# Ways into two expert mixtures: clearing, spreading, selection and turned rows in another order

## The chip, the cores and the metric

The kernel runs on one core of one Trainium2 chip, in one launch. The metric is the device time of that launch in microseconds (us). The kernel before takes 2220.22 us, the median of three runs (2218.92 to 2225.36).

## The reference, cut to what matters

The input is 256 tokens of width 1024, all in float32. A first block has two layers: sparse attention with a dense feed-forward part, then block-wise attention with a mixture of 8 experts (width 3584, two chosen per token). A second block follows: an mLSTM and Fourier mixer, and a mixture of 16 experts (width 512, two chosen per token out of one group of four). What the change touches is how tokens get to their experts:

```python
logits = (xf @ w_router).astype(F32)                 # first mixture; the second adds a group choice
vals, idx = lax.top_k(logits, TOP_K_EXPERTS)
w = jax.nn.softmax(vals, axis=-1)
for e in range(N_EXPERTS):
    y = y + gate[:, e:e + 1].astype(xf.dtype) * swiglu(xf, wg[e], wu[e], wd[e])
...
x = x + gate2 * rmsnorm_2(hier_moe(h2, lp), g_post_ffn[l])
```

## The kernel before, in words

Activations are held transposed: 8 tiles of 128 channels by 256 tokens (`hT` is the residual stream, `uT` the normed input). Weights stream from HBM through six ring slots of 2 MB, all issued by SyncE in one fixed order. Every engine runs its own hand-written order, and they meet in semaphores.

A helper pair hands results from TensorE (PE) to the engine that takes them: `open_job` gives TensorE one of the five PSUM banks 1 to 5 in rotation, and waits until the job five before has been taken; `next_job` is the taker's side. `copy_job` is ScalarE's (ACT) copy of such a bank. `settle` makes TensorE wait until all jobs so far are taken.

The way into a mixture (`routing(m, X)`, for m = 0 and 1) is, on TensorE: four jobs `byt` of four transposes each (the normed tokens as rows, `by_token`); in the second mixture four more jobs `hR` (the residual `hT` turned to rows, `rows_h`, for the output's last step); then the job `rank` (five small matmuls that count the tokens ahead of each within its expert), for which VectorE (DVE) must have found the choices (`s_a`); then, when VectorE has the slot of each token (`s_lg`), two jobs `gr` of four matmuls each. The first spreads the slot columns `cols[54:58]` over the partitions, and ScalarE copies it to `grow`; the second spreads the weights `cols[46:50]`, for `wrow`. Then TensorE settles, and `zero_sums` clears the four banks 4 to 7, in which all outputs of the mixture are summed, by four matmuls with zeros.

VectorE meanwhile runs `top2`: choices, softmax weights, ranks, slots (up to L1917, `s_lg`), then the table of which expert each tile of slots belongs to (L1921 to L1929, `s_tab`). Then it enters the mixture: it copies the slot number (L1776, L1816) and makes `selection`, the 0/1 matrix `pick` (L1759, L1762) with which TensorE gathers the tokens of a tile (`gather`, L756). In the second mixture it then clears two tiles (L1818, L1819).

The mixture itself loops over tiles of slots (96 wide in the first, 64 in the second). Before its loop, TensorE waits for `s_tab` and `M.sel` and gathers; ScalarE and VectorE copy the gathered inputs to `xg` (`inputs`, L1410 and L1766); TensorE clears the two banks of the tile's own output (`clear_y`, L770, first mixture only) and starts on the gate weights (L776, or L870 in the second). Each of the first mixture's tiles takes seven chunks of 6 MB of weights, twelve granules each; SyncE loads a granule of the next chunk when TensorE is through with the one in its place. The second mixture's tiles take one chunk of 6 MB in three loads, each issued when the same slot's weights have been used. The first chunk of both is loaded ahead. SyncE, TensorE, ScalarE and VectorE each read the number of tiles from the table with `value_load`.

Ahead of the second mixture's router stand two norms in a row: squares by ScalarE, sums by TensorE (L518), root by ScalarE (L1318), reciprocal (L1625) and scaling (L1620) by VectorE, shift by ScalarE (L1331), and the router's matmuls (L713).

Of the kernel before, what the change touches and what calls it, by code (L numbers as in the profile page):

```python
# [14 lines left out]
P = 128  # L15
# [3 lines left out]
NT = T // P  # L19
# [55 lines left out]
def program(nc, A, out):  # L75
    with ExitStack() as ctx:
# [3 lines left out]
        def sem(name):  # L80
            return ctx.enter_context(nc.semaphore(name))
# [159 lines left out]
        s_top = sem("top_found"); s_e = sem("top_exponential"); s_lg = sem("gates_by_token")  # L241
        s_a = sem("choices_ready"); s_tab = sem("tables_ready")
# [224 lines left out]
        def _(pe):  # L467
# [232 lines left out]
            def zero_sums():  # L700

                for i in range(4):
                    pe.matmul(psum[:, 4 + i, :], zeros[:], pk("causal"), start=True, stop=False,
                              skip_group_check=True)

# [11 lines left out]
            def routing(m, X):  # L717
# [9 lines left out]
                if m == 1:  # L727
                    pe.wait_ge(s_hT, 28)
                    for t in range(NT):
                        for g in range(2):  # L730
                            b, _ = open_job(pe, "hR", "A")
                            for k in range(4):
                                mm = pe.transpose(b[:, P * k:P * k + P], hT[:, 4 * g + k, P * t:P * t + P], ident)
                            mm.then_inc(res, 1)
# [8 lines left out]
                pe.wait_ge(s_lg, m + 1)  # L743
                for o in (54, 46):
                    b, _ = open_job(pe, "gr", "A")
                    for q in range(4):
                        mm = pe.matmul(b[:, P * q:P * q + P], cols[:, o + q:o + q + 1].to_broadcast([P, P]), ident,
                                       start=True, stop=True)
                    mm.then_inc(res, 1)
# [11 lines left out]
            def first_mixture():  # L761
# [5 lines left out]
                def clear_y():  # L767

                    for i in range(2):
                        pe.matmul(psum[:, 2 + i, 0:4 * N], zeros[:], pk("causal")[:, 0:4 * N], start=True, stop=False,  # L770
                                  skip_group_check=True)
# [68 lines left out]
            def second_mixture():  # L840
# [16 lines left out]
                pe.wait_ge(s_tab, 2)  # L857
                pe.wait_ge(M.sel, 1)
                pe.wait_ge(*mark["byt"][-1])
                gather(M)  # L860
                last = pe.value_load(M.tab[0:1, TABLE:TABLE + 1], min_val=0, max_val=TABLE - 2)
# [236 lines left out]
            settle()  # L1098
            zero_sums()
# [180 lines left out]
            norm()  # L1280
            router(uT, "router2", 20, 56)
            routing(1, uT)
            settle()
            zero_sums()
# [18 lines left out]
        def _(act):  # L1303
# [18 lines left out]
            def h_pairs(v):  # L1322

                return lambda i: (s_hT, 4 * v - 3 + i)
# [69 lines left out]
            def routing(m):  # L1394
# [7 lines left out]
                if m == 1:  # L1402
                    for t in range(NT):
                        for g in range(2):
                            copy_job("hR", rows_h[:, t, 512 * g:512 * g + 512], lambda b: b)
                for dst in (grow, wrow):
                    copy_job("gr", dst, lambda b: b)
# [8 lines left out]
            def first_mixture():  # L1416
                M = mix[0]
                N, CH = M.N, M.CH
                last = act.value_load(M.tab[0:1, TABLE:TABLE + 1], min_val=0, max_val=TABLE - 2)
                act.wait_ge(M.gath, 1)  # L1420
                inputs(M)
                with act.Fori(0, last + 1) as q:
# [12 lines left out]
            def second_mixture():  # L1435
                M = mix[1]
                act.sem_inc(M.yA, 1)
                last = act.value_load(M.tab[0:1, TABLE:TABLE + 1], min_val=0, max_val=TABLE - 2)
                act.wait_ge(M.gath, 1)
                inputs(M)  # L1440
                with act.Fori(0, last + 1) as q:
# [76 lines left out]
            act.wait_ge(s_tab, 1)  # L1518
# [60 lines left out]
            norm(hT, h_pairs(7))  # L1579
# [918 lines left out]
```

## Time and profile before

| what | value |
|---|---|
| median of three runs | 2220.22 us |
| the profiled execution, its own time | 2222.7 us |
| its span in the profile | 2220.7 us |
| PE busy | 2059.9 us, 93% |
| DVE busy | 596.2 us, 27% |
| ACT busy | 406.2 us, 18% |
| DMA | 640.83 MB, mean 289 GB/s |
| mean granted TensorE clock | 0.964 of full |

Some 1.5 us or more lie outside the span: the profiled execution's own time is 2.0 us above it. Times in the timelines are us from the start of the span. A line of the timeline is start, duration, engine, line of the kernel, operation, what is written and read, the number of instructions merged in it, and in brackets how long the engine had been idle before and what released it. PE is TensorE's array, PEld its weight load, SPq SyncE's queue. The granted clock is a share of 2.4 GHz: 1.00 is the upper level, 0.50 the lower (1.2 GHz).

### The profile page before, as it was taken

How to read it: one execution, taken by the hardware profiler on the slowest of the kernel's cores; microseconds unless marked ns; L12 is line 12 of the kernel's file. 1: busy time of each engine (PE TensorE's matmuls, PEld its weight loads, DVE VectorE, ACT ScalarE, POOL GpSimd, SP SyncE). 2: the span in 40 equal slices, each digit the busy share in tenths (PEclk: the TensorE clock that was granted, in tenths of full speed). 3: DMA queues.
4: the chain of work that ended last, by engine and by line, in shares of the span. 5: the costliest groups of instructions: out<-in, count | busy, mean ns of one | idle time of the engine just before them, and what ended most of it. 6: DMA issues, size and time to landing. Idle time of an engine off the chain costs nothing.

```text
span 2220.7 us, 75430 instructions
## 1 busy us (share of the span) xinstructions
PE 2059.9 (93%) x34412; PEld 1794.6 (81%) x34412; DVE 596.2 (27%) x1360; ACT 406.2 (18%) x812; POOL 11.9 (1%) x20
## 2 busy tenths in 40 slices
PE   4979999999999999999999999999988987899998
PEld 2767888888548899999898989898977776777776
DVE  2577734241452201010101010101015252322222
ACT  2142000021463111011111111111112422211111
POOL 0000000000010000000000000000000000000000
PEclk8999999999899899999999999999999998999999
DMA  8717988914565599999999999999990110599995
GB/s 320 271 68 260 337 315 300 318 46 152 187 231 206 194 395 334 393 338 396 383 396 393 392 394 391 395 391 395 390 387 22 55 39 0 201 411 401 407 401 240
DMA packets 253306, 640.83 MB, mean 289 GB/s; under 512 B 15152, under 2 KB 21424, under 8 KB 247984
## 3 DMA queue, kind: packets, MB, share of 16 engines
q1 hardware_dynamic: 252384, 634.93, 76.1%
q10 hardware_dynamic: 848, 4.84, 0.6%
q8 instruction: 54, 0.88, 0.2%
q14 instruction: 20, 0.16, 0.0%
HBM read 638.68 MB, written 1.05 MB: 288 GB/s over the span
## 4 chain that ended last, share of the span: by engine, by line
PE 70%; DMA 20%; DVE 5%; SPq 2%; ACT 2%; issue 1%; DVEq 0%; POOLq 0%; POOL 0%; ACTq 0%
PE psum L776 23%; DMA ring<-in_moe_w_up 13%; PE psum L534 8%; DMA ring<-in_w_up 5%; PE psum L676 4%; PE psum L661 3%; PE psum L685 3%; PE psum L879 3%; PE psum L756 2%; SPq L2322 2%; PE psum L870 2%; PE psum L893 1%; PE psum L544 1%; PE psum L494 1%; PE psum L829 1%; PE psum L1275 1%
## 5 line engine op out<-in xcount | busy, mean ns | idle before, releaser
L776 PE MATMUL psum<-uT,ring 128*64 128x80 f32 (+1 forms) x14336 | 564.1, 237 | 23.9 <-DMA ring<-in_moe_w_up 21.6
L776 PEld LDWEIGHTS psum<-uT,ring 128*64 128x64 f32 x14336 | 532.4, 137 | 53.7 <-DMA ring<-in_moe_w_up 37.4
L776 PE MATMUL psum<-arena,ring 128*64 128x80 f32 (+1 forms) x7168 | 269.5, 236 | 0.0
L776 PEld LDWEIGHTS psum<-arena,ring 128*64 128x64 f32 x7168 | 264.0, 137 | 0.0
L1799 DVE TENSOR_TENSOR arena<-arena,psum 128x288 f32<-128x288 f32 x56 | 25.4, 454 | 729.7 <-PE psum L776 729.7
L1426 ACT ACTIVATE arena<-psum 128x384 f32<-128x384 f32 x56 | 27.6, 492 | 697.2 <-PE psum L776 697.2
L1645 DVE SCALAR_TENSOR_TENSOR arena<-ring,cact,arena 128x512 f32<-128x512 f32 x168 | 126.3, 752 | 5.7
L534 PE MATMUL psum<-uT,ring 128*128 128x256 f32 (+1 forms) x496 | 113.5, 389 | 3.9 <-ACT uT L1331 3.6
L534 PEld LDWEIGHTS psum<-uT,ring 128*128 128x128 f32 (+1 forms) x496 | 95.3, 194 | 22.0 <-issue 7.8
L534 PE MATMUL psum<-arena,ring 128*128 128x256 f32 x384 | 87.1, 389 | 4.9 <-ACT arena L1331 3.6
L534 PEld LDWEIGHTS psum<-arena,ring 128*128 128x128 f32 x384 | 74.4, 195 | 16.3 <-issue 3.9
L870 PEld LDWEIGHTS psum<-uT,ring 128*64 128x64 f32 x2432 | 73.8, 138 | 15.5 <-issue 14.7
L676 PE MATMUL psum<-uT,ring 128*128 128x256 f32 x352 | 79.5, 385 | 3.6 <-ACT uT L1331 3.6
L879 PE MATMUL psum<-uT,ring 128*64 128x64 f32 x2432 | 74.9, 223 | 6.0 <-DMA ring<-in_w_up 5.9
L676 PEld LDWEIGHTS psum<-uT,ring 128*128 128x128 f32 x352 | 68.0, 193 | 13.5 <-issue 4.0
L879 PEld LDWEIGHTS psum<-uT,ring 128*64 128x64 f32 x2432 | 72.5, 138 | 7.4 <-DMA ring<-in_w_up 7.4
L685 PE MATMUL psum<-uT,ring 128*128 128x256 f32 x352 | 77.8, 379 | 0.0
L870 PE MATMUL psum<-uT,ring 128*64 128x64 f32 x2432 | 74.5, 222 | 3.5 <-DMA ring<-in_w_gate 2.8
L661 PE MATMUL psum<-arena,ring 128*128 128x256 f32 x352 | 77.6, 379 | 0.0
L1307 ACT ACTIVATE arena<-psum 128x512 f32<-128x512 f32 (+2 forms) x61 | 33.7, 552 | 228.8 <-PE psum L534 111.7
L661 PEld LDWEIGHTS psum<-arena,ring 128*128 128x128 f32 x352 | 66.9, 190 | 9.1
L685 PEld LDWEIGHTS psum<-uT,ring 128*128 128x128 f32 x352 | 66.9, 190 | 9.1
(420 smaller groups left out, 2047.7 us busy)
## 6 DMA issues: line engine op xcount, KB each, us to landing
ring<-in_moe_w_gate SPq DMA_DIRECT2D x224, 512.0 KB, 11.0
ring<-in_moe_w_up SPq DMA_DIRECT2D x224, 512.0 KB, 10.1
ring<-in_moe_w_down SPq DMA_DIRECT2D x224, 512.0 KB, 11.1
ring<-in_w_ada SPq DMA_DIRECT2D x36, 2048.0 KB, 14.2
ring<-in_w_up SPq DMA_DIRECT2D x19, 2048.0 KB, 11.1
ring<-in_w_down SPq DMA_DIRECT2D x19, 2048.0 KB, 10.0
ring<-in_w_gate SPq DMA_DIRECT2D x19, 2048.0 KB, 10.5
ring<-in_ffn_w_gate SPq DMA_DIRECT2D x5, 2048.0 KB, 7.8
```

Source lines behind the costliest of these rows:

```text
L534: mm = pe.matmul(b[0:rows, T * j:T * j + T], wt[:, k, c0 + P * j:c0 + P * j + rows], X[:, k, :], start=(k == 0), stop=(k == kt - 1))
L661: mm = pe.matmul(psum[:, 4 + j // 2, T * (j % 2):T * (j % 2) + T], down.w[:, 2 * (h % 2) + f, P * j:P * j + P], hid[:, h % 2, f, :], start ...
L676: mm = pe.matmul(psum[:, h % 2, T * f:T * f + T], ffn.g[:, k, 256 * (h % 2) + P * f:256 * (h % 2) + P * f + P], X[:, k, :], start=(k == 0) ...
L685: mm = pe.matmul(psum[:, 2 + h % 2, T * f:T * f + T], ffn.u[:, k, 256 * (h % 2) + P * f:256 * (h % 2) + P * f + P], X[:, k, :], start=(k = ...
L756: mm = pe.matmul(psum[HD * hc:HD * hc + HD, k // 4, N * (k % 4):N * (k % 4) + N], by_token[:, t, P * k + HD * hc:P * k + HD * hc + HD], M. ...
L776: mm = pe.matmul(out(HD * hc), w[:, c0 + HD * hc:c0 + HD * hc + HD], x, skip_group_check=True, **kw)
L870: mm = pe.matmul(psum[HD * hc:HD * hc + HD, 0, N * f:N * f + N], w[:, k, o:o + HD], M.xg[:, k, :], start=(k == 0), stop=(k == KT - 1), ski ...
L879: mm = pe.matmul(psum[HD * hc:HD * hc + HD, 1, N * f:N * f + N], w[:, k, o:o + HD], M.xg[:, k, :], start=(k == 0), stop=(k == KT - 1), ski ...
L1307: act.activation(dst, view(b), ACT.Copy).then_inc(act_took, 1)
L1426: act.activation(M.silu[:, 0, :], psum[:, 0, 0:4 * N], ACT.Silu).then_inc(M.sg, 1)
L1645: V(stt(acc, w[:, k, :], cact[:, k:k + 1], acc, ALU.mult, ALU.add), s_acc if k == KT - 1 else None)
L2322: sp.dma_start(dst, w.rearrange("e (k p) n -> p (e k) n", p=P)).then_inc(M.land[i], 16)
```

## The change

- `routing` on TensorE: after the rank job it settles; the weights (`wrow`) are spread first, without a wait for `s_lg`, into bank 3; then it waits for `s_lg` and spreads the slots (`grow`) into bank 2. They are no jobs any more; two new semaphores `s_gr` and `s_grt` pass them.
- `zero_sums` goes. ScalarE clears banks 4 to 7 by four copies of zeros, once the `byt` and `rank` jobs are taken (`s_zero`).
- In `top2` the slot number and `selection` come right after `s_lg`, ahead of the table.
- The wait for `s_tab` moves behind the first gather on TensorE, behind the first `inputs` on ScalarE. VectorE waits for `s_grt` on entering.
- `clear_y` is split: bank 2 is cleared ahead of the wait for the inputs, bank 3 behind it.
- The four `hR` jobs of the second mixture move from `routing` to between the second norm's sums and the router; ScalarE's copies of them stand between the root and the shift of that norm.

```diff
@@ routing, TensorE
-                if m == 1:
-                    pe.wait_ge(s_hT, 28)
-                    ... (four hR jobs; now behind the second norm(), ahead of router())
                 pe.wait_ge(s_a, m + 1)
                 b, _ = open_job(pe, "rank", "V")
...
-                pe.wait_ge(s_lg, m + 1)
-                for o in (54, 46):
-                    b, _ = open_job(pe, "gr", "A")
+                settle()
+                for bank, o in ((3, 46), (2, 54)):
+                    if o == 54:
+                        pe.wait_ge(s_lg, m + 1)
                     for q in range(4):
-                        mm = pe.matmul(b[:, P * q:P * q + P], cols[:, o + q:o + q + 1].to_broadcast([P, P]), ident,
+                        mm = pe.matmul(psum[:, bank, P * q:P * q + P], cols[:, o + q:o + q + 1].to_broadcast([P, P]), ident,
                                        start=True, stop=True)
-                    mm.then_inc(res, 1)
+                    mm.then_inc(s_gr, 1)
@@ both mixtures, TensorE
-                pe.wait_ge(s_tab, 1)
                 pe.wait_ge(M.sel, 1)
                 pe.wait_ge(*mark["byt"][-1])
                 gather(M)
+                pe.wait_ge(s_zero, 1)
+                pe.wait_ge(s_grt, 2)
+                pe.wait_ge(s_tab, 1)
                 def tile(q, W):
+                    clear_y(0)
                     pe.wait_ge(M.xgA, q + 1)
                     pe.wait_ge(M.xgV, q + 1)
-                    clear_y()
+                    clear_y(1)
@@ before both mixtures, TensorE
-            settle()
-            zero_sums()
@@ routing, ScalarE
-                if m == 1:
-                    ... (four hR copies; now behind norm(hT, h_pairs(7)))
-                for dst in (grow, wrow):
-                    copy_job("gr", dst, lambda b: b)
+                act.wait_ge(*mark["byt"][4 * m + 3])
+                act.wait_ge(*mark["rank"][m])
+                for i in range(4):
+                    ins = act.activation(b3(psum[:, 4 + i, :], 4), bc(zeros[:], 4), ACT.Copy)
+                ins.then_inc(s_zero, 1)
+                for i, (bank, dst) in enumerate(((3, wrow), (2, grow))):
+                    act.wait_ge(s_gr, 2 * m + i + 1)
+                    act.activation(dst, psum[:, bank, :], ACT.Copy).then_inc(s_grt, 1)
@@ both mixtures, ScalarE (s_tab 2 in the second)
-                last = act.value_load(...)
                 act.wait_ge(M.gath, 1)
                 inputs(M)
+                act.wait_ge(s_tab, 1)
+                last = act.value_load(...)
@@ both mixtures, VectorE (s_grt 4 in the second)
-                V(dve.tensor_copy(slot_no, pk("part")))
-                selection(M, V)
                 dve.sem_inc(M.s, 1)
+                dve.wait_ge(s_grt, 2)
@@ top2, VectorE, behind s_lg
+                V(dve.tensor_copy(slot_no, pk("part64" if m else "part")))
+                selection(M, V)
```

## Rows read from the trace of the kernel before

**Rows 1.** The page: shares of the chain that ended last, by line.
```profile
PE psum L776 23%; DMA ring<-in_moe_w_up 13%; PE psum L534 8%; DMA ring<-in_w_up 5%; PE psum L676 4%; PE psum L661 3%; PE psum L685 3%; PE psum L879 3%; PE psum L756 2%; SPq L2322 2%; PE psum L870 2%; PE psum L893 1%; PE psum L544 1%; PE psum L494 1%; PE psum L829 1%; PE psum L1275 1%
```

**Rows 2.** Windows of two tiles: length, PE, PEld, DVE, ACT, POOL busy, PEclk, DMA, GB/s.
```profile
860.00:972.10 112.10, 112.10 (x2620) 110.87 (x2622) 7.13 (x21) 12.18 (x14) 0.00 (x0) 1.00 0.97 364
...
1196.30:1308.40 112.10, 107.27 (x2782) 101.67 (x2778) 9.07 (x25) 14.00 (x17) 0.00 (x0) 1.00 1.04 392
```

**Rows 3.** Windows, second mixture from its third tile to its last load.
```profile
1942.30:2192.20 249.90, 241.09 (x5634) 192.98 (x5630) 61.64 (x176) 42.69 (x65) 0.00 (x0) 1.00 0.99 404
```

**Rows 4.** Timeline of the way into the first mixture.
```profile
725.07 0.18 DVE L1892 TENSOR_SCALAR small<-psum 128x24 f32<-128x24 f32 x1 [1.88 <-PE psum L742]
...
728.88 3.78 PE L747 MATMUL psum<-pack,cols 128*128 128x128 f32 x16 [3.92 <-DVE cols L1917]
...
731.37 0.15 DVE L1929 TENSOR_SCALAR posi<-small 128x1 int32<-128x1 f32 x1
...
732.23 0.55 DVE L1762 SCALAR_TENSOR_TENSOR score<-pack,cols,score 128x96 f32<-128x96 f32 x2
732.70 0.60 ACT L1307 ACTIVATE arena<-psum 128x512 f32<-128x512 f32 x1 [1.11 <-PE psum L747]
...
733.35 5.92 PE L703 MATMUL psum<-pack,zeros 128*128 128x512 f32 x8 [0.69 <-ACT arena L1307]
...
739.20 2.86 PE L756 MATMUL psum<-score,sq 128*64 128x96 f32 x64
...
742.90 1.53 PE L770 MATMUL psum<-pack,zeros 128*128 128x384 f32 x4 [0.84 <-DVE uT L1766]
...
744.36 10.78 PE L776 MATMUL psum<-uT,ring 128*64 128x96 f32 x256
```

**Rows 5.** Windows on both ways in: the granted clock stands third from the end.
```profile
723.00:726.00 3.00, 1.96 (x11) 1.86 (x9) 0.91 (x6) 1.46 (x4) 0.00 (x0) 0.50 0.00 0
...
737.00:739.20 2.20, 2.20 (x6) 0.69 (x4) 0.00 (x0) 0.00 (x0) 0.00 (x0) 0.81 0.00 0
...
1900.00:1902.00 2.00, 1.62 (x8) 1.33 (x7) 1.65 (x7) 0.89 (x2) 0.00 (x0) 0.55 0.01 4
```

**Rows 6.** Timeline of the way into the second mixture.
```profile
1873.51 1.75 DVE L1625 RECIPROCAL rstd<-root 128x256 f32<-128x256 f32 x1 [6.95 <-ACT root L1318]
...
1875.82 3.31 ACT L1331 ACTIVATE uT<-uT,mods 128x256 f32<-128x256 f32 x8 [2.34 <-DVE uT L1620]
...
1876.47 6.82 PE L713 MATMUL psum<-pack,uT 128*128 128x20 f32 x32 [3.51 <-ACT uT L1331]
...
1888.76 0.19 DVE L1882 TENSOR_TENSOR small<-small 128x32 f32<-128x32 f32 x1
1888.87 3.64 ACT L1307 ACTIVATE sq<-psum 128x512 f32<-128x512 f32 x4
...
1892.31 2.08 ACT L1307 ACTIVATE ring<-psum 128x512 f32<-128x512 f32 x4
...
1892.65 0.58 PE L738 MATMUL psum<-small,pack 128*128 128x16 f32 x2
...
1897.60 0.19 DVE L1917 TENSOR_REDUCE cols<-small 128x2 f32<-128x32 f32 x1
...
1897.84 3.78 PE L747 MATMUL psum<-pack,cols 128*128 128x128 f32 x16 [2.90 <-DVE cols L1917]
...
1899.70 0.15 DVE L1929 TENSOR_SCALAR posi<-small 128x1 int32<-128x1 f32 x1
...
1901.57 0.91 DVE L1819 MEMSET arena<- 128x1024 f32 x1 [0.28 <-DVE prob L1818]
...
1905.94 2.09 PE L756 MATMUL psum<-score,sq 128*64 128x64 f32 x64
...
1908.65 3.95 PE L870 MATMUL psum<-uT,ring 128*64 128x64 f32 x128 [0.62 <-DVE uT L1766]
...
1912.78 0.36 SPq L2362 DMA_DIRECT2D ring<-in_w_gate  x1
```

More of the change, by code:

```diff
@@ L241, in program @@
         s_top = sem("top_found"); s_e = sem("top_exponential"); s_lg = sem("gates_by_token")
+        s_gr = sem("slot_rows_in"); s_grt = sem("slot_rows_taken"); s_zero = sem("sums_cleared")
         s_a = sem("choices_ready"); s_tab = sem("tables_ready")
@@ L698, in settle @@
                 pe.wait_ge(dve_took, taken["V"])
[L700 to L704, printed above, removed]
             def router(X, w, E, base):
@@ L726, in routing @@
                         mm.then_inc(res, 1)
-                if m == 1:
-                    pe.wait_ge(s_hT, 28)
[L729 to L733, printed above, removed]
-                            mm.then_inc(res, 1)
                 pe.wait_ge(s_a, m + 1)
@@ L765, in first_mixture, with clear_y @@
                 wd = slot_view(M.slots[2], 4, D)
[L767 to L771, printed above, removed]
+                def clear_y(i):
+                    pe.matmul(psum[:, 2 + i, 0:4 * N], zeros[:], pk("causal")[:, 0:4 * N], start=True, stop=False,
+                              skip_group_check=True)
                 def block(out, w, x, c0, **kw):
@@ L860, in second_mixture @@
                 gather(M)
+                pe.wait_ge(s_zero, 2)
+                pe.wait_ge(s_grt, 4)
+                pe.wait_ge(s_tab, 2)
                 last = pe.value_load(M.tab[0:1, TABLE:TABLE + 1], min_val=0, max_val=TABLE - 2)
@@ L1280, in _ @@
             norm()
+            for t in range(NT):
+                for g in range(2):
+                    b, _ = open_job(pe, "hR", "A")
+                    for k in range(4):
+                        mm = pe.transpose(b[:, P * k:P * k + P], hT[:, 4 * g + k, P * t:P * t + P], ident)
+                    mm.then_inc(res, 1)
             router(uT, "router2", 20, 56)
             routing(1, uT)
-            settle()
-            zero_sums()
             second_mixture()
@@ L1401, in routing @@
                             copy_job("byt", spread, lambda b: b.rearrange("p (n k) -> p n k", k=KT))
-                if m == 1:
-                    for t in range(NT):
-                        for g in range(2):
-                            copy_job("hR", rows_h[:, t, 512 * g:512 * g + 512], lambda b: b)
-                for dst in (grow, wrow):
-                    copy_job("gr", dst, lambda b: b)
+                act.wait_ge(*mark["byt"][4 * m + 3])
[6 more added lines that the diff above has]
+                    act.activation(dst, psum[:, bank, :], ACT.Copy).then_inc(s_grt, 1)
             def inputs(M):
@@ L1437, in second_mixture @@
                 act.sem_inc(M.yA, 1)
-                last = act.value_load(M.tab[0:1, TABLE:TABLE + 1], min_val=0, max_val=TABLE - 2)
                 act.wait_ge(M.gath, 1)
                 inputs(M)
+                act.wait_ge(s_tab, 2)
+                last = act.value_load(M.tab[0:1, TABLE:TABLE + 1], min_val=0, max_val=TABLE - 2)
                 with act.Fori(0, last + 1) as q:
@@ L1579, in _ @@
             norm(hT, h_pairs(7))
+            for t in range(NT):
+                for g in range(2):
+                    copy_job("hR", rows_h[:, t, 512 * g:512 * g + 512], lambda b: b)
             shift(uT, M2(3, 0), s_norm)
@@ L1815, in second_mixture @@
                 S = 2 * N
-                V(dve.tensor_copy(slot_no, pk("part64")))
-                selection(M, V)
+                dve.wait_ge(s_grt, 4)
                 V(dve.memset(M.selG[0:S, :], 0.0))
```

6 lines of the change are left out of this document (1 added, 5 removed).

## The prediction, made before the changed kernel was timed

> **What bounds the kernel now.** I read the chain of waits first. Its largest lines are the expert matmuls of the first mixture (L776, 23%) and the weights they wait for (`in_moe_w_up`, 13%); the second mixture's loads `in_w_up` have 5% [rows 1]. None of the lines the change edits has 1% there except the gather L756 (2%, nearly all of it inside the loops), so nothing is to be had from the bulk of the time: the question is only whether the two mixtures start earlier, and whether an earlier start reaches the end.
>
> For that I cut windows of one tile each. A wide tile of the first mixture takes 112.1 us with TensorE busy for all of them. A narrow one takes the same 112.1 us with TensorE busy for 107.3 and the DMA share at 1.04 [rows 2]. So the first two tiles (the wide ones; one row of them stands) are TensorE's, the other six the weight stream's, and the stream of chunk n+1 is released by TensorE's use of chunk n. Neither has a fixed clock time of its own. The second mixture is the stream's from its third tile on: DMA share 0.99 over 249.9 us [rows 3]. Its stream starts when the first gate pass is done: SyncE's first load inside the loop issues at 1912.78, 4.13 us behind the start of that pass at 1908.65 [rows 6]. Both are rigid bodies: shift the first matmul by x and the end shifts by x. The time between the mixtures is TensorE's and its helpers', with weights loaded ahead, and shifts with them.
>
> That leaves the timelines of the two ways in.
>
> **First mixture, before** [rows 4]. VectorE has the slots at 728.86. From there on TensorE alone is the path: both spreads (3.78 us, so 1.89 each), ScalarE's copy of the second, the zeros (5.92), the gather (2.86), 0.84 us of waiting for the inputs, the clear of two banks (1.53), and the first expert matmul at 744.36. That is 744.36 - 728.88 = 15.48 us.
>
> **First mixture, after.**
> - The spread of the weights needs only the rank job taken (VectorE at 725.07, done 725.25). It lies at 725.3 to 727.2, where TensorE now waits for the slots. Off the path: -1.89.
> - The copy and settle behind the second spread (732.66 to 733.35: 0.69) go from TensorE's path. ScalarE copies `grow` while TensorE gathers.
> - The zeros on TensorE go: -5.92.
> - ScalarE's four clears: the trace has no ScalarE write into PSUM. The nearest rows are its copies of 512 columns, 0.60 us [rows 4], and the strided ones at 3.64/4 = 0.91 [rows 6]. So 2.4 to 3.6 us, and I take 2.4, since source and target lie in runs of 128, as the cheaper copies' do. They start at 725.3, end at 727.7 (at most 729), and the `wrow` copy follows. TensorE asks for them at the end of the gather, behind 733. Cost nothing; below nothing is excluded, as nobody gains by a clear.
> - Selection ahead of the table: from 731.52 to 732.78 in the trace, 1.26 us, now 728.9 to 730.1, so it is there before TensorE has finished the slot spread at 730.8. The table moves back by the same 1.26, to 732.8. TensorE, ScalarE and SyncE ask for it only behind the gather (733.6 at the earliest), SyncE first needs it for a load behind the first matmuls. What hides it is the gather; without that cover it would cost 1.26.
> - TensorE now gathers at 730.8. Then the 0.84 us gap, in which one half of the clear is to fit, and the other half, 0.77, behind it.
>
> Sum at the upper clock for the gather: 1.89 + 2.86 + 0.84 + 0.77 = 6.4 us instead of 15.48, a gain of 9.1.
>
> **The clock.** Here I don't trust that sum. The granted clock is 0.50 from 723 on and rises in the window 737.00 to 739.20, whose mean 0.81 puts the rise at 737.8 [rows 5]. The zeros ran through that rise: in the old order they did the warming, and the gather came behind it. In the new order the gather stands at 730.8. At the lower clock it takes 5.7, so it would end at 736.5, the first half clear falls in the gap, and the second ends near 738.4: a gain of 6.0. TensorE is busier between 725 and 729 than before, which speaks for an earlier rise; I take 7.5, the middle of 6.0 and 9.1. The Trainium skill ("TensorE: Matmul & The Clock Gate", Part 1: The HAM clock gate) says that the clock is withheld by default and released by TensorE's recent activity; the trace agrees in direction (0.50 behind idle stretches, 1.00 behind the zeros), and by that rule alone one would expect taking useless matmuls away to cost part of what it saves.
>
> **Ahead of the second mixture: the hR jobs.** TensorE idles 3.51 us between the second norm's sums and the router [rows 6]; four jobs of four transposes fit in it: sixteen passes of the same 128x128 shape took 3.78 us at the lower clock [rows 4 to 6], so they take 1.9 at the upper and 3.8 at the lower. ScalarE's four copies are 4 x 0.60 = 2.4 us, from the end of the root (1873.5) on; its shift can't start before 1875.82 anyway (reciprocal 1.75, first scaling 0.5), 2.3 us later. So it costs nothing to 0.1 us if TensorE delivers at the upper clock, and up to 1.3 if it delivers at the lower and the shift is late. In return TensorE's idle stretch is shorter, and the router's 6.82 us, part of them at the lower clock, may shrink by up to 3. Bounds -1.3 and +3; I take a gain of 0.3, near the nothing that the row's own slack gives.
>
> **Second mixture, before** [rows 6]. The choices `s_a` are ready at 1888.95, but the rank job starts at 1892.65. Between them stood the hR jobs, waiting for banks, which ScalarE frees only from 1888.87 on (four copies of 0.91). From 1892.65 to the slots at 1897.79 are 5.14 us, and from there to the gate pass at 1908.65 10.86.
>
> **Second mixture, after.**
> - Rank starts at 1889.0: its bank was the router's, long taken. Gain 3.65. The slots are ready at 1894.15.
> - What is late next is ScalarE. Its four `byt` copies end at 1892.51, and `settle` waits for them. The weight spread lies at 1892.55 to 1894.45, which is 0.3 us beyond the slots; the slot spread ends at 1896.35.
> - ScalarE's clears start at 1892.5 and end at 1894.9 (1896.1 at the dearer bound); `wrow` is copied by 1895.5 and `grow` by 1897.0 (1897.3).
> - VectorE: selection to 1895.4, table to 1897.5 (1899.85 - 1897.79 = 2.06 behind it), then the wait for `grow`, and its two clears (from the table to their end it was 1902.48 - 1899.85 = 2.63, less the selection's 1.26: 1.4), to 1898.9.
> - Gather from 1896.4, 2.09 at the upper clock, 4.2 at the lower, to 1898.5 or 1900.5. The gate pass starts 0.62 later, 1899.1 or 1901.2. Before, the clock rose near 1901.8, 4 us behind the start of the spreads (the window 1900 to 1902 has 0.55 [rows 5]); now the spreads start at 1892.6.
>
> Gain 9.6 or 7.5; I take 8.5. Register reads of the table now come just behind its writing on VectorE. No row prices one alone. They are inside the 0.84 and 0.62 us gaps before the first matmul, so 0 to 0.8 us each way in; with the middle taken for the clock I leave it in the range.
>
> **The sum.** 7.5 + 0.3 + 8.5 = 16.3 us. The profiled execution's own time, 2222.7, becomes 2206.4. It is 2.5 us above the median of the runs shown, and inside their range. From the median, 2220.22 - 16.3 = 2203.9; I say 2204.
>
> **Rivals.**
> 1. *The lower clock eats the gather and more.* Mechanism: TensorE without its zeros rises no earlier than before (737.8), and in the second way in the gather and part of the first gate pass run at 0.50. For: both ways in run at 0.50 today. Against: the busy stretch begins earlier. Gains 6.0 and 6.5, and -0.7 for a late shift: 11.8 in all, 2208.4. Chance 25%.
> 2. *The upper clock everywhere.* The weight spread and the hR jobs fill idle stretches and the clock is up for both gathers and part of the router: 9.1 + 9.6 + 2 = 20.7, 2199.5. Chance 15%.
> 3. *It doesn't do what it says.* Something else holds the mixtures' start, as a weight chunk that lands late: then the earlier TensorE waits. Against: no DMA moves in the windows 723 to 726 and 737 to 739 [rows 5], so the first chunk lies there; SyncE's own read of the table has until 736. For the whole gain to fall under 6.7 us, 10 of 16 would have to be lost. 2216. Chance 6%.
> 4. *Slower: the stream.* After the shift the weight stream of either mixture runs at another phase to TensorE's releases. There are 55 chunks behind the first in the first mixture and 18 in the second, 73 at some 16.0 us (112.1 / 7). If each takes 0.22 us more, the gain is gone; at 0.35 us more the kernel takes 2220.2 - 16.3 + 25.6 = 2229.5. For it speaks only that three runs of one program differ by 6.4 us; against it, that both tiles shown, wide and narrow, take 112.1 us, and the six narrow ones (of which one row stands) all do. Chance 4%.
>
> The forecast itself (13 to 19 us) has 50%. The range: the clock's bounds give 2199.5 to 2208.4, the register reads and the dearer clears another 2, and the median of three runs may sit 2 us off; 2198.5 to 2211.5 leaves out rival 3, most of 4 and little else.
>
> A difference of 0.3%, 6.7 us, is about what a measurement of this kernel can tell from none. Faster by more: 50 + 25 + 15 = 90%, less 1 for luck in the runs. Within: 6%, and 1 from there. Slower: 4%.
>
> **What the profile after would show.** L703 is gone; ScalarE has four copies of 0.6 us from zeros at 725.3; L747's second half starts at 728.9, the gather at about 730.9, the first expert matmul between 735.3 and 738.4. In the second way in the rank job starts at 1889.0 less the first gain, followed 3.5 us later by the first spread, and the gate pass comes 10.1 to 12.2 us behind the rank's start instead of 16.0. Tiles stay at 112.1, and the second mixture's 249.9 stays. The forecast is wrong if the first matmul comes later than 739, if the shift of the second norm starts over 1 us later behind its root, or if either stretch of tiles changes by over 3 us.

## The result, and the profile after

The changed kernel takes 2204.76 us (median of six runs, 2198.64 to 2206.11) against 2221.22 us before it, six runs on the same chip. The ratio is 0.9922, with a 95% interval of 0.9906 to 0.9938: 17.3 us faster, or 13.8 to 20.9. The forecast was 2204 us. A second set of the same two kernels, taken later, gave 2209.26 against 2220.38, ratio 0.9944 (0.9928 to 0.9960). Two sets of this one program differ by 4.5 us, so the parts below are read from spans inside single profiles. The spans of the two ways in repeat within 0.05 us in the two profiles of the changed kernel; the long stretch of unchanged work between them does not (1128.9 and 1131.4 us).

The timeline of the changed kernel on the first way in answers to [rows 4] (columns as there):

```profile
723.64 2.16 ACT L1399 ACTIVATE psum<-zeros 128x512 f32<-128x512 f32 x4 [0.88 <-DVE small L1889]
...
723.70 2.05 PE L735 MATMUL psum<-pack,cols 128*128 128x128 f32 x8 [0.44 <-DVE small L1889]
...
726.95 0.17 DVE L1914 TENSOR_REDUCE cols<-small 128x2 f32<-128x16 f32 x1
...
727.17 2.08 PE L735 MATMUL psum<-pack,cols 128*128 128x128 f32 x8 [1.42 <-DVE cols L1914]
...
727.82 0.55 DVE L1761 SCALAR_TENSOR_TENSOR score<-pack,cols,score 128x96 f32<-128x96 f32 x2
...
729.17 4.88 PE L744 MATMUL psum<-score,sq 128*64 128x96 f32 x64
729.28 0.60 ACT L1403 ACTIVATE arena<-psum 128x512 f32<-128x512 f32 x1 [2.90 <-PE psum L735]
...
730.79 0.15 DVE L1928 TENSOR_SCALAR posi<-small 128x1 int32<-128x1 f32 x1
...
734.10 0.56 DVE L1765 COPY uT<-psum 128x384 f32<-128x384 f32 x1 [3.16 <-PE psum L744]
...
734.59 1.53 PE L757 MATMUL psum<-pack,zeros 128*128 128x384 f32 x4 [0.54 <-issue]
...
736.04 10.78 PE L763 MATMUL psum<-uT,ring 128*64 128x96 f32 x256
```

The weight spread (L735, first) and ScalarE's four clears (L1399, 2.16 us in all) lie beside VectorE's chain. From the slots at 727.12 TensorE does the slot spread, the gather (L744) and the clear, and starts on the experts (L763) at 736.04: 8.92 us, where it was 15.54 (744.36 less VectorE's end of the slots, 728.82). The gather takes 4.88 us instead of 2.86 [rows 4]. The windows of the changed kernel show why (granted clock third from the end):

```profile
727.20:729.10 1.90, 1.90 (x8) 1.75 (x8) 1.79 (x7) 0.00 (x0) 0.00 (x0) 0.50 0.03 9
729.10:732.00 2.90, 2.90 (x37) 2.83 (x38) 1.64 (x7) 0.60 (x1) 0.00 (x0) 0.50 0.00 0
732.00:734.10 2.10, 2.05 (x33) 1.86 (x30) 0.00 (x0) 0.00 (x0) 0.00 (x0) 0.67 0.00 0
734.10:736.10 2.00, 1.51 (x6) 0.73 (x7) 1.93 (x7) 1.36 (x2) 0.00 (x0) 1.00 0.01 4
```

The clock is at its lower level until 733.4 (worked out from the mean 0.67 of the third window, taking one rise in it), 6.3 us behind the slots, so most of the gather runs at 1.2 GHz.

The timeline of the second way in, against [rows 6]:

```profile
1864.74 1.91 PE L1275 MATMUL psum<-pack,hT 128*128 128x128 f32 x16
1864.94 0.48 ACT L1312 ACTIVATE root<-psum,epsc 128x256 f32<-128x256 f32 x1 [4.24 <-PE psum L519]
1865.37 2.07 ACT L1301 ACTIVATE ring<-psum 128x512 f32<-128x512 f32 x4
...
1867.75 3.31 ACT L1325 ACTIVATE uT<-uT,mods 128x256 f32<-128x256 f32 x8 [0.31 <-DVE uT L1619]
...
1868.40 6.79 PE L708 MATMUL psum<-pack,uT 128*128 128x20 f32 x32 [1.76 <-ACT uT L1325]
...
1880.77 3.62 ACT L1301 ACTIVATE sq<-psum 128x512 f32<-128x512 f32 x4
...
1880.91 0.61 PE L725 MATMUL psum<-small,pack 128*128 128x16 f32 x2 [2.22 <-DVE small L1879]
...
1884.44 3.78 PE L735 MATMUL psum<-pack,cols 128*128 128x128 f32 x16 [1.22 <-ACT sq L1301]
...
1888.15 3.13 PE L744 MATMUL psum<-score,sq 128*64 128x64 f32 x64
...
1889.02 0.15 DVE L1928 TENSOR_SCALAR posi<-small 128x1 int32<-128x1 f32 x1
...
1889.85 0.91 DVE L1816 MEMSET arena<- 128x1024 f32 x1 [0.28 <-DVE prob L1815]
1891.33 0.38 ACT L1406 ACTIVATE uT<-psum 128x256 f32<-128x256 f32 x1 [2.48 <-PE psum L744]
1891.69 0.42 DVE L1765 COPY uT<-psum 128x256 f32<-128x256 f32 x1 [0.93 <-PE psum L744]
...
1892.26 3.95 PE L862 MATMUL psum<-uT,ring 128*64 128x64 f32 x128 [0.98 <-DVE uT L1765]
```

The hR transposes and ScalarE's copies of them end before the shift can start, which begins 2.81 us behind the root as before (2.82). The rank job (L725) follows the choices at once. From it to the gate pass (L862) are 11.35 us instead of 16.00. From the root to the gate pass it is 27.32 instead of 35.65.

One account for the whole profile, before less after (spans 2220.7 and 2202.6): up to the slots of the first way 1.70, the first way 6.62, from the first expert matmul to the second norm's root -0.26, from there to the gate pass 8.33, the rest 1.71; sum 18.10. The change's own two stretches make 14.95 of it. The other 3.15 us are unchanged work in another execution: over the profiles of all versions below with the same code there, the slots of the first way come at 726.1 to 730.1 us, and the stretch from the first expert matmul to the root takes 1125.2 to 1131.4. Windows of the same lengths as in [rows 2, 3] show nearly the same work done:

```profile
1188.00:1300.10 112.10, 107.27 (x2782) 101.69 (x2780) 9.06 (x25) 14.00 (x17) 0.00 (x0) 1.00 1.04 392
...
1926.00:2175.90 249.90, 241.63 (x5654) 193.58 (x5650) 61.63 (x176) 42.64 (x65) 0.00 (x0) 1.00 1.00 405
```

### The profile page after: what moved, and what is told of

The parts are those of the page before. It is cut to its first block, busy times and chain, and to the rows that moved or that the text cites. A ratio compares the mean times of both kernels' runs of the same rounds, so it can differ in the third digit from the quotient of the medians.

```text
span 2202.6 us, 75416 instructions
## 1 busy us (share of the span) xinstructions
PE 2050.2 (93%) x34396; PEld 1791.4 (81%) x34396; DVE 596.0 (27%) x1360; ACT 410.9 (19%) x820; POOL 11.9 (1%) x20
## 4 chain that ended last, share of the span: by engine, by line
PE 70%; DMA 19%; DVE 6%; SPq 2%; ACT 2%; issue 1%; DVEq 0%; POOLq 0%; POOL 0%
PE psum L763 23%; DMA ring<-in_moe_w_up 13%; PE psum L535 8%; DMA ring<-in_w_up 5%; PE psum L677 4%; PE psum L662 3%; PE psum L686 3%; PE psum L871 3%; PE psum L744 2%; PE psum L862 2%; SPq L2321 2%; PE psum L885 2%; PE psum L1116 1%; PE psum L1265 1%; PE psum L819 1%; PE psum L495 1%
## 5 line engine op out<-in xcount | busy, mean ns | idle before, releaser
L763 PE MATMUL psum<-uT,ring 128*64 128x80 f32 (+1 forms) x14336 | 565.0, 237 | 23.8 <-DMA ring<-in_moe_w_up 21.5
L763 PEld LDWEIGHTS psum<-uT,ring 128*64 128x64 f32 x14336 | 532.6, 137 | 54.3 <-DMA ring<-in_moe_w_up 37.5
L763 PE MATMUL psum<-arena,ring 128*64 128x80 f32 (+1 forms) x7168 | 269.4, 236 | 0.0
L763 PEld LDWEIGHTS psum<-arena,ring 128*64 128x64 f32 x7168 | 263.8, 137 | 0.0
L862 PEld LDWEIGHTS psum<-uT,ring 128*64 128x64 f32 x2432 | 73.8, 138 | 15.0 <-issue 13.9
L862 PE MATMUL psum<-uT,ring 128*64 128x64 f32 x2432 | 74.5, 222 | 2.9 <-DMA ring<-in_w_gate 1.7
```

Source lines behind the costliest of these rows:

```text
L763: mm = pe.matmul(out(HD * hc), w[:, c0 + HD * hc:c0 + HD * hc + HD], x, skip_group_check=True, **kw)
L862: mm = pe.matmul(psum[HD * hc:HD * hc + HD, 0, N * f:N * f + N], w[:, k, o:o + HD], M.xg[:, k, :], start=(k == 0), stop=(k == KT - 1), ski ...
```

## The experiments

All are variations of the changed kernel. The columns: the first way from the slots (end of the second slot reduction) to the first expert matmul; the second way from the norm's root (start) and from the rank job (start) to the gate pass; the median, its runs, and the ratio to the kernel before in the same set, where several runs were made. Each span comes from one profile. Whole times from different sets do not tell versions 2 to 5 us apart: the interval of the changed kernel's ratio, 0.9906 to 0.9938, overlaps or touches that of every other version, and the single runs say less still. The spans carry the argument.

| kernel | first way | root to gate | rank to gate | us (runs) | ratio |
|---|---|---|---|---|---|
| before | 15.54 | 35.65 | 16.00 | | |
| changed | 8.92 | 27.32 | 11.35 | 2204.76 (6) | 0.9922 |
| changed, again | 8.97 | 27.29 | 11.35 | 2209.26 (6) | 0.9944 |
| zeros on TensorE | 12.77 | 30.47 | 14.47 | 2210.44 (6) | 0.9954 |
| hR behind byt | 8.96 | 31.15 | 11.32 | 2210.94 (4) | 0.9953 |
| selection late | 10.99 | 28.75 | 12.76 | 2204.22 (1) | |
| spreads together | 9.89 | 28.78 | 12.85 | 2211.69 (1) | |
| table first | 10.82 | 27.31 | 11.35 | 2206.57 (1) | |
| clears early | 8.96 | 26.98 | 11.01 | 2203.34 (1) | |
| three orders | 8.97 | 25.52 | 9.56 | 2206.20 (4) | 0.9934 |
| TensorE busy | 7.14 | 25.54 | 10.85 | 2203.52 (4) | 0.9920 |
| orders and busy | 7.13 | 25.54 | 10.85 | 2202.27 (6) | 0.9925 |
| the same, trimmed | 7.40 | 23.26 | 8.42 | 2199.77 (5) | 0.9913 |

**Zeros on TensorE.** They go back behind the two spreads, and ScalarE's clears go.

```diff
+                for i in range(4):
+                    pe.matmul(psum[:, 4 + i, :], zeros[:], pk("causal"), start=True, stop=False,
+                              skip_group_check=True)
...
-                for i in range(4):
-                    ins = act.activation(b3(psum[:, 4 + i, :], 4), bc(zeros[:], 4), ACT.Copy)
-                ins.then_inc(s_zero, 1)
```

> The changed kernel, but TensorE clears the four sum banks again, now between the slot spread and the gather; ScalarE's four clears go. Theory (the zeros warm the clock, so part of what their removal saves is paid back in the gather): the gather falls from 4.88 to about 2.9 us in the first way in and from 3.13 to 2.1 in the second, and from the slots to the first expert matmul the first way takes 8.87 + 5.5 - 2.0 = 12.4 us, the second, from the rank job on, 11.35 + 3.7 - 1.0 = 14.0. In all +6.1 on the changed kernel's 2204.8, 2211. Rival (the zeros were plain length, the clock rises when it rises): +5.9 and +3.7, 14.8 and 15.0 us, 2214.4.

Measured: 12.77 and 14.47 us. Its timeline:

```profile
728.43 5.73 PE L739 MATMUL psum<-pack,zeros 128*128 128x512 f32 x8
...
734.08 2.86 PE L747 MATMUL psum<-score,sq 128*64 128x96 f32 x64
...
737.81 1.53 PE L760 MATMUL psum<-pack,zeros 128*128 128x384 f32 x4 [0.87 <-issue]
```

The zeros cost 5.73 us and the gather behind them is back at 2.86. The Trainium skill ("TensorE: Matmul & The Clock Gate", Part 1: The HAM clock gate) has the clock released by activity, and the pair agrees: useless matmuls ahead, a faster gather behind (2.86 us for 4.88). They don't bring the rise forward, though: the windows put it 6.2 us behind the slots here (728.43 to 734.08 has a mean of 0.62) and 6.3 in the changed kernel. They fill the time at the lower clock that the gather otherwise spends there. The price can be read from the gather's start: without the zeros it comes 5.53 us earlier behind the slots (2.05 for 7.58), and from there to the clear (L757, here L760) it takes 1.69 us more (5.42 for 3.73). That leaves the 3.85 us of the table.

In the first way the theory's 12.4 holds and the rival's 14.8 doesn't; in the second 14.47 lies midway between 14.0 and 15.0, and only the gather's 2.09 speaks for the theory. The whole is 5.7 us over the changed kernel's first set (forecast 6.1), but 1.2 over its second, and decides nothing.

**hR behind the byt jobs.** On TensorE the four jobs stand ahead of the wait for the choices again, on ScalarE the four copies behind those of `byt`.

```diff
+                if m == 1:
+                    pe.wait_ge(s_hT, 28)
+                    for t in range(NT):
+                        for g in range(2):
+                            b, _ = open_job(pe, "hR", "A")
...
                 pe.wait_ge(s_a, m + 1)
...
-            for t in range(NT):
-                for g in range(2):
-                    b, _ = open_job(pe, "hR", "A")
...
             router(uT, "router2", 20, 56)
...
+                if m == 1:
+                    for t in range(NT):
+                        for g in range(2):
+                            copy_job("hR", rows_h[:, t, 512 * g:512 * g + 512], lambda b: b)
```

> The changed kernel, but the four hR jobs stand again between the byt jobs and the rank job on TensorE, and behind the byt copies on ScalarE. Theory (they hold the rank job for banks, and cost nothing in the norm): the rank job starts 3.6 us later behind the choices, the gate pass 3.6 us later behind the second norm's root, router and shift unchanged within 0.2; 2208.4. Rival (what they save behind the router they cost ahead of it, by ScalarE's late shift): the shift starts 1 to 2 us earlier behind the root than in the changed kernel, and the whole is worth 1 to 2 us; 2206.5.

Measured: root to gate 31.15, 3.83 us longer, all of it ahead of the rank job (rank to gate 11.32). The shift starts 2.81 us behind the root, as in both other kernels, so the jobs cost nothing where the change puts them. The theory holds; the rival doesn't.

**Selection late, spreads together, table first.** Three orders of the change, each undone alone: the selection moved behind the table (first hunk), both spreads behind the slots (second), and TensorE's wait for the table ahead of the gather (third).

```diff
-                V(dve.tensor_copy(slot_no, pk("part64" if m else "part")))
-                selection(M, V)
...
-                for bank, o in ((3, 46), (2, 54)):
+                for bank, o in ((2, 54), (3, 46)):
...
+                pe.wait_ge(s_tab, m + 1)
                 gather(M)
```

> The changed kernel, but slot number and selection come behind the table again. Theory: the gather waits for the selection. In the first way in it starts at the table's end plus 1.3 us, that is 1.9 us later behind the slots (8.87 becomes 10.8); in the second VectorE's own order has the same length, only the gather starts 1.2 us later, and the gate pass about 0.85 us later (11.35 becomes 12.2). Together +2.7, 2207.5 us. Rival (the place of the selection is free, TensorE's spreads cover both orders): 8.9 and 11.4, 2204.8 us.

> The changed kernel, but both spreads wait for the slots, the slot columns first. Theory (the early weight spread takes 1.9 us off the path in the first way, and in the second too, since ScalarE's late byt copies hold it only 1.2 us): from the slots to the first expert matmul 8.87 becomes 10.8 to 11.5, from the rank job to the gate pass 11.35 becomes 13.1; 2208.7 us. Rival (in the second way it is worthless, because ScalarE's copies held both spreads): 10.8 and 11.4.

> The changed kernel, but TensorE waits for the table ahead of the first gather of each mixture, as before the change. Theory (the table, moved behind the selection, would then hold the gather: it is ready 3.8 us behind the slots where the slot spread ends 2.0 behind them; in return the register reads are hidden and half the clear falls into the wait for the inputs): the first way 8.9 becomes 10.3, the second 11.35 becomes 11.9; 2206.7 us. Rival (the reads' 0.5 us is no longer paid and the gather meets the upper clock, so the place of this wait is free): 9.0 and 11.4.

Measured: selection late +2.07 and +1.41 (forecast 1.9 and 0.85). Its first way:

```profile
730.48 5.39 PE L744 MATMUL psum<-score,sq 128*64 128x96 f32 x64 [1.88 <-DVE score L1761]
...
735.92 1.60 PE L757 MATMUL psum<-pack,zeros 128*128 128x384 f32 x4
```

Spreads together +0.97 and +1.50, where the first way was to lose at least 1.9. Here the cause can be read in its timeline:

```profile
728.75 3.75 PE L735 MATMUL psum<-pack,cols 128*128 128x128 f32 x16 [4.00 <-DVE cols L1914]
...
732.43 3.72 PE L744 MATMUL psum<-score,sq 128*64 128x96 f32 x64
```

The gather comes 1.8 us later behind the slots than in the changed kernel but meets the clock's rise in its middle and takes 3.72 instead of 4.88. (In the second way VectorE waits 1.62 us for the second copy before its clears.) Table first costs 1.90 in the first way (forecast 1.4) and nothing in the second, where the forecast said 0.55. There the rival was right. Its gather did meet the upper clock, as the rival has it (2.09 us), but that isn't why the way is no longer: VectorE, not the gather, holds the inputs, as the repeated run below shows.

Read together, the three show what sets the clock's rise. The gather starts equally late behind the slots in all of them (4.0, 3.8 and 4.0 us). With both spreads running up to it the rise comes 5.6 us behind the slots. With TensorE idle for 1.9 us ahead of it (selection late, table first) the rise comes only 9.6 and 9.0 us behind them, and the gather takes 5.39 and 5.29 us, nearly all at the lower clock. So the gather's place alone doesn't decide; the later rise goes with TensorE's idling. These times are worked out from the mean clock of windows, one profile each.

**Clears early, and three orders.** The first kernel moves VectorE's two clears from the entry of the second mixture to ahead of its wait for the rank job. The second moves also ScalarE's `byt` copies (`rows`) ahead of the second exponential of the choices, and VectorE's first inputs ahead of its read of the table.

```diff
+                if m == 1:
+                    V(dve.memset(M.selG[0:2 * N, :], 0.0))
+                    V(dve.memset(rows_by_slot[0:2 * N, :], 0.0))
                 b = next_job(dve, "rank", "V")
...
-                V(dve.memset(M.selG[0:S, :], 0.0))
-                V(dve.memset(rows_by_slot[0:S, :], 0.0))
...
+            rows(1)
             act.wait_ge(s_top, 3)
...
-                last = dve.value_load(M.tab[0:1, TABLE:TABLE + 1], min_val=0, max_val=TABLE - 2)
                 dve.wait_ge(M.gath, 1)
                 inputs(M)
+                last = dve.value_load(M.tab[0:1, TABLE:TABLE + 1], min_val=0, max_val=TABLE - 2)
```

> The changed kernel, but VectorE's two clears of the second mixture stand ahead of its wait for the rank job, in idle time. Theory (VectorE, by its clears and the table read behind them, holds the second way's inputs for 0.36 us behind the gather): inputs start right at the gather's end, from the rank job to the gate pass 11.0 instead of 11.35 us, nothing else. Rival (the read of the table's register holds the inputs, not the clears): 11.35 stays.

> The changed kernel with three orders changed and nothing added: VectorE's two clears ahead of its wait for the rank job, ScalarE's four byt copies of the second way ahead of the wait for the top exponential, and VectorE's first inputs ahead of its read of the table. Theory (behind the change the second way is bound by the slots at the lower clock, not by ScalarE or VectorE): the rank job to the gate pass takes 10.7 instead of 11.35, the first way stays at 8.9; 2204.1 us. Rival (ScalarE's byt copies still held the whole second way in by 1 us): 9.7 us, 2203.1 us.

Measured: the clears alone 11.01, as forecast. The three orders 9.56, near the rival's 9.7, but only in part for its reason. Of the 1.45 us between the two, 0.4 come from the gather's earlier start behind the slots (1.67 for 2.10), which ScalarE's late byt copies had held, and 1.0 from a gather that meets the upper clock (2.09 for 3.12). Whether the early weight spread brought that rise forward isn't shown by one profile: the repeated run of the changed kernel, without these orders, had it too:

```profile
1893.36 2.09 PE L744 MATMUL psum<-score,sq 128*64 128x64 f32 x64
...
1895.33 0.91 DVE L1816 MEMSET arena<- 128x1024 f32 x1 [0.28 <-DVE prob L1815]
...
1897.74 3.95 PE L862 MATMUL psum<-uT,ring 128*64 128x64 f32 x128 [2.30 <-DVE uT L1765]
```

> The changed kernel itself, beside the trimmed one on the same chip. Theory: both ways in as in its first profile, 8.9 us from the slots and 11.35 from the rank job, within 0.3, since only the clock's rise can differ; 2204 to 2206 us. Rival (the ways in vary from run to run as much as the whole does): either differs by over 1 us.

In that run the gather met the upper clock (2.09 instead of 3.13), and the way is 11.35 us again, to the hundredth: TensorE just waits 2.30 us for VectorE. The bound of the changed second way is VectorE's chain of selection, table, clears, the step with the register read (the 0.93 us ahead of its inputs at 1891.69) and inputs: from the slots to the inputs it takes 5.61 us in both profiles, and in that of table first too. The length of the gather is not part of it.

**TensorE busy.** Matmuls of zeros into bank 0, whose next writer is the gather: one of 128 columns per pass of both routers, full ones ahead of the second router, ahead of the rank jobs and between the spreads.

```diff
+            def busy(n, w=512):
+                for _ in range(n):
+                    pe.matmul(psum[:, 0, 0:w], zeros[:], pk("causal")[:, 0:w], start=True, stop=True,
+                              skip_group_check=True)
...
+                        if t == 0:
+                            busy(1, P)
...
+                busy(3 if m else 1)
                 pe.wait_ge(s_a, m + 1)
...
+                        busy(0 if m else 2)
                         pe.wait_ge(s_lg, m + 1)
...
+            busy(2)
             router(uT, "router2", 20, 56)
```

> The changed kernel, with matmuls of zeros into the unused bank 0 wherever TensorE idles on both ways in: two of 512 columns ahead of the second router, one of 128 columns behind each of the first eight passes of both routers, one and three of 512 ahead of the rank jobs, two between the two spreads of the first way. Theory (the lower clock comes from TensorE's gaps and thin matmuls, and costs the routers, spreads and gathers): the granted clock stays at 1.00 through both ways in, the router's matmuls fall from 6.8 to about 5 us, the spreads from 3.8 to 1.9 in the second way, the gathers from 4.88 and 3.13 to 2.9 and 2.1; the first way gains 4 to 5 us and the second 4, 2196 us. Rival (the lower clock isn't to be avoided by a few matmuls): the added matmuls run at 0.50 themselves and delay the path by 3 to 6 us, 2209 us.

Measured: neither. From the slots on, the first way takes 7.14 us (there the table ends last: the clear starts 1.86 us behind it), but the router ahead of them takes 9.2 us where it took 6.8: the clock falls there all the same, and the added matmuls run at it. The windows of this kernel (granted clock third from the end), from the router's start to behind the slots:

```profile
712.00:713.50 1.50, 1.50 (x12) 1.50 (x13) 1.50 (x5) 1.50 (x5) 0.00 (x0) 0.90 0.05 18
713.50:726.00 12.50, 12.50 (x55) 11.67 (x55) 4.97 (x30) 4.39 (x9) 0.00 (x0) 0.50 0.48 181
726.20:728.00 1.80, 1.50 (x11) 1.41 (x9) 0.18 (x1) 0.00 (x0) 0.00 (x0) 0.82 0.00 0
728.00:730.00 2.00, 1.86 (x11) 1.41 (x12) 1.56 (x11) 1.91 (x4) 0.00 (x0) 1.00 0.00 0
```

The means of the first and third put the fall at 713.2 and the rise at 726.8. The second way's clock holds through the router, the transposes and the zeros (1.00 in windows from 1864 to 1880.1). Then it falls again: the window 1880.10 to 1887.14 has 0.78, and the spreads take 3.53 us. The way gains 1.78:

```profile
1872.57 1.86 PE L713 MATMUL psum<-pack,uT 128*128 128x20 f32 x16
1874.27 1.94 PE L727 MATMUL psum<-pack,uT 128*128 128x128 f32 x16
```

These are the second half of the router and the byt transposes at the upper clock; the latter took 3.65 us in the changed kernel.

> The same three orders, and TensorE kept busy with matmuls of zeros into bank 0: in the second way two of 512 columns ahead of the router, one of 128 behind each of its first eight passes, three ahead of the rank job, two between the spreads; in the first way only one of 384 between the spreads. Theory (the lower clock costs the second way its router, rank job, spreads and gather, and in the first way half of the gather): from the second norm's root to the gate pass 22.2 us instead of 27.3, in the first way 7.9 from the slots instead of 8.9; 2198.7 us. Rival (the table and its register reads take the place of what the clock gave): 24.5 and 8.9, 2202 us.

Measured: the first way 7.13 (forecast 7.9), the second 25.54 instead of the forecast 22.2. Two of its own steps held it: VectorE's clears, now in a gap that had become too short, delayed its taking of the rank job by 1.1 us, and the two added matmuls between the spreads ran at the lower clock (3.35 us) and held the slot spread 1.7 us behind the slots.

> The version with three orders changed and TensorE kept busy, trimmed: VectorE's two clears ahead of its wait for the second router (they had held its taking of the rank job), and one matmul of zeros between the second way's spreads instead of two (they had held the slot spread 1.7 us). Theory (with the clock up, the way is bound by VectorE's table and TensorE's register reads): from the second norm's root to the gate pass 22.9 us instead of the changed kernel's 27.3, the first way 7.1 from the slots as in the untrimmed version; 6 us under the changed kernel run beside it. Rival (the clock falls in TensorE's short waits again, so the spreads and the gather are at the lower clock): 25 us, 4 us under it.

Measured: 7.40 and 23.26 us, forecast 7.1 and 22.9. Its gather in the second way starts 1.2 us behind the slots and takes 2.09. The gate pass starts 0.99 us behind the start of VectorE's inputs, where it is 0.57 in the changed kernel, so TensorE's own reads of the table probably end last; that is argued, not shown. It has the lowest median: 2199.77 us, ratio 0.9913 (0.9895 to 0.9930), beside 0.9944 (0.9928 to 0.9960) for the changed kernel in the same set; the two intervals just overlap. The two spans account for 5.6 of the 9.5 us between them.

## Why the prediction was right

The total was right within 1 us, in part by luck: 14.95 us come from the change's two stretches where 16.3 were forecast, and unchanged work in this execution made up for it. The second set, at 2209.26 us, lies 5 us above the forecast, though inside its range. By its own steps:

- *Both mixtures are rigid bodies.* Right as far as the profiles tell. From the first expert matmul to the second norm's root 1128.64 us before and 1128.90 after; that they agree so closely is luck, as this stretch spreads over 6 us in the other profiles. The stream rival, which needs 16 us, is out: the rest behind the gate pass is 310.3 against 312.1 us, not longer. One reading was wrong: 112.1 us is the length of the windows [rows 2], not of a wide tile. From one input copy of VectorE to the next the second wide tile takes 120.49 us in both kernels, the last five narrow ones 112.0 to 112.4 before and 111.9 to 113.1 after. TensorE is busy all through the wide one's window, so the argument stands.
- *First way 7.5 of 6.0 to 9.1.* Measured 6.62. The spread, the slots and ScalarE's clears (2.16 us for the 2.4 I took) came as worked out. The largest mis-sized term is the gather: 4.88 us, nearer the 5.7 of the lower clock, where the middle I took meant 4.3. The idea behind it was right, as the zeros put back on TensorE show: they made the gather cheap. The clock rose 6.3 us behind the slots, where it was 9.0 before (737.8), but so late in the gather that only its last part gained. The next step cost another 0.4 us. (The lower bound of 6.0 is 6.3 by its own terms: 736.5 + 0.84 + 0.77 is 738.1, not 738.4.)
- *Half of the first clear falls into the wait for the inputs.* Wrong. Both halves run in a row (734.59 to 736.04), so gap and clear take 1.99 us where 0.84 + 0.77 were forecast. The step that failed is the reading of the 0.84 us in [rows 4] as a wait for the inputs. With the zeros on TensorE the first clear waits for no inputs, and the table has been ready for 7.5 us, yet it starts 0.87 us behind a gather of the same 2.86, on issue (TensorE waits for nothing that the profile shows). So that time is TensorE's own and hides nothing. It isn't simply a delay behind the gather either: in seven profiles with gathers of 4.58 to 5.39 us (the changed kernel twice, hR behind byt, selection late, table first, clears early, three orders) the clear starts 5.39 to 5.45 us behind the gather's start (4.60 behind that of spreads together, whose gather took 3.72). A gather shorter by 0.24 us in the repeated run (4.64) brought nothing, and the way took 8.97. What in TensorE's instruction stream sets this, the register reads or something else, stays open: the reads alone weren't varied.
- *hR in the norm costs nothing; 0.3 gained by a warmer router.* The cost is right, the gain isn't there: the router takes 6.79 us, as before (6.82). It needed two added matmuls ahead and one per pass to keep the clock.
- *The rank job 3.65 us earlier.* Right: 3.83 by putting hR back.
- *Second way 8.5 of 7.5 to 9.6, by the clock.* Measured 8.33 from the root on, rank to gate 11.35, inside the forecast 10.1 to 12.2. But what ended last was not what I worked with. VectorE's inputs start 0.4 us behind the gather, because of its clears and the 0.93 us with the register read, which I had put at 0 to 0.8 and off the sum. The prediction had the numbers to see it: it puts the end of VectorE's clears at 1898.9, already behind the faster gather's end at 1898.5, and then adds 0.62 to the gather. From 1898.9, the 0.93 us and the 0.57 from inputs to gate pass give 1900.4, 11.4 us behind the rank job at 1889.0; it is 11.35. In the repeated run the gather was 1 us shorter and nothing came of it. A right size with the wrong last term.
- Rival 1 (the lower clock, 11.8 in all) describes the first way, not the second. Rivals 2, 3 and 4 did not occur.

What each part is worth, by undoing it alone: zeros off TensorE 3.85 + 3.15 us, hR moved 3.83, selection ahead of the table 2.07 + 1.43, weights spread early 0.97 + 1.46, the wait for the table behind the gather 1.90 + 0. The sum is 18.7, over the 14.95 of all together. One reason can be read: selection late and table first both put the gather's start 2 us back, so each counts the same cover.

## What to carry to other kernels

Taking filler work off an idle-prone TensorE path is paid back in part by whatever dense work follows at the lower clock (1.7 of 5.5 us here); price the follower at both levels before counting the filler as gain. A gap ahead of an instruction is cover only if it is a wait for what the new order still waits for: here 0.84 us read as a wait for inputs was TensorE's own. When a wait is shortened, list every engine's arrival at the next meeting point with its register reads and clears: here the slack between TensorE and VectorE was 0.4 to 2.3 us, and it decided what further savings were worth. Where single sets of runs move by 4 us, measure a change of 15 us by the spans of its own stretches in several profiles, and don't read the unchanged stretches as evidence below their own spread (6 us here).

## What the runs showed of the hardware

In the changed second way 0.93 us lie on VectorE between its clear and its inputs, with the table's register read, two semaphore increments and a wait in them; the figure is the same in three profiles. With the read moved behind the inputs (three orders) a gap of 0.46 us stands there instead, so the read alone isn't priced.

On TensorE the first clear starts 1.86 and 1.85 us behind the table where the table comes last (TensorE busy, orders and busy), with two register reads between them. The gap behind the gather doesn't follow the table: it is 0.87 us where the table was ready long before (zeros on TensorE), 0.5 to 0.9 where it came during the gather, 0.05 and 0.10 behind the two gathers that ran nearly all at the lower clock.

In a thin stretch (the first router, 8 columns per pass) matmuls of zeros between its passes did not keep the clock up: it fell 1.2 us into the router and was 0.50 from 713.2 to 726.8, though TensorE counts as busy in all of the window 713.50 to 726.00. In the second router, with two full matmuls ahead, the same filling kept the upper level; in the changed kernel, without both, the window 1868.40 to 1875.20 has 0.62.

ScalarE's copy of a zero tile into PSUM, 128 x 512, took 0.54 us each; the Trainium skill ("ScalarE: Activation LUTs", What ACT_TABLE_LOAD costs) gives 186 ns and 0.833 ns per column, less 93 ns of overlap back to back, an estimate of 0.52 for 512 columns, and the trace agrees.
